# A two-block transformer kernel on one core: the on-chip tensors are stored in another order

## The reference, cut to what matters

```python
act = gelu(einsum('td,ted->te', hx, u_sel))      # u_sel = peer_u[idx]
out = einsum('te,ted->td', gate * act, v_sel)    # v_sel = peer_v[idx]
```

## The kernel before, in words

| tensor | byte | remainder by 256 |
|---|---|---|
| ring | 16,544 | 160 |
| weights_hi | 32,928 | 160 |
| more_lo | 80,032 | 160 |
| u_lo | 162,976 | 160 |
| v_lo, first block | 212,176 | 208 |
| work | 198,752 | 96 |
| small | 206,944 | 96 |
| h | 212,064 | 96 |
| hh | 220,256 | 96 |

## Time and profile before

### The profile page before, as it was taken

The page is one execution under the profiler, slowest core; times in us unless marked ns, Lnnn a source line. Parts: engine busy times, 40 slices in busy tenths (PEclk is TensorE's granted clock), DMA queues, the critical chain, the costliest instruction groups (busy, mean ns, idle before and its releaser), DMA issues.

```text
span 3314.2 us, 71368 instructions
## 1 busy us (share of the span) xinstructions
PE 3191.5 (96%) x28224; PEld 3071.2 (93%) x28224; DVE 2522.3 (76%) x4560; ACT 1604.3 (48%) x2581; POOL 197.1 (6%) x331
## 2 busy tenths in 40 slices
PE   6999989999999999899999999999899999999998
PEld 6999769999967998889999999998789999999998
DVE  7989667988835896748978867776756978877776
ACT  4466644454544445234455444444425455554444
POOL 1100001111100110200000000000400000000000
PEclk9999999999999999999999999999899999999999
DMA  9965218979721993156775477775226885567774
GB/s 392 390 225 168 75 45 329 388 292 371 265 87 49 406 359 124 41 172 201 232 213 171 149 249 235 235 237 167 84 87 193 243 238 174 174 211 236 235 236 161
DMA packets 246737, 707.30 MB, mean 213 GB/s; under 512 B 27488, under 2 KB 93024, under 8 KB 245456
## 3 DMA queue, kind: packets, MB, share of 16 engines
q1 hardware_dynamic: 212256, 572.17, 52.1%
q0 software_dynamic: 34224, 131.55, 10.4%
HBM read 669.00 MB, written 34.60 MB: 212 GB/s over the span
## 4 chain that ended last, share of the span: by engine, by line
PE 88%; DVE 5%; DMA 3%; ACT 2%; issue 1%; SPq 0%; POOL 0%; DVEq 0%; POOLq 0%; ACTq 0%
PE psum L584 39%; PE psum L616 29%; PE psum L1138 3%; PE psum L1073 1%; PE psum L713 1%; DMA ring<-stream 1%; PE psum L965 1%; PE psum L555 1%; PE psum L988 1%; DMA arena<-mod_weights 1%; PE psum L595 1%; PE psum L761 1%; DVE ring L1730 1%; PE psum L596 1%; PE psum L880 1%
## 5 line engine op out<-in xcount | busy, mean ns | idle before, releaser
L584 PE MATMUL psum<-hh,weights_hi 128*128 128x256 f32 x4216 | 1190.1, 282 | 20.0 <-ACT arena L1429 8.5
L584 PE MATMUL psum<-h,weights_hi 128*128 128x256 f32 x4216 | 1175.2, 279 | 0.0
L584 PEld LDWEIGHTS psum<-hh,weights_hi 128*128 128x128 f32 x4216 | 798.1, 189 | 26.6 <-issue 11.2
L584 PEld LDWEIGHTS psum<-h,weights_hi 128*128 128x128 f32 x4216 | 796.8, 189 | 0.2
L616 PE MATMUL psum<-small,weights_hi 128*128 128x256 f32 x2752 | 770.0, 280 | 4.6 <-DVE ring L1730 4.6
L616 PE MATMUL psum<-work,weights_hi 128*128 128x256 f32 x2752 | 768.3, 279 | 0.0
L1730 DVE TENSOR_TENSOR ring<-ring,weights_hi 128x1024 fp32r<-128x1024 f32 x463 | 566.1, 1225 | 184.6 <-ACT weights_hi L1212 180.7
L1212 ACT ACTIVATE weights_hi<-ring 128x1024 fp32r<-128x1024 f32 x463 | 488.3, 1056 | 373.2 <-PE psum L616 182.2
L584 PE MATMUL psum<-hh,ring 128*128 128x256 f32 x2016 | 563.6, 280 | 0.0
L616 PEld LDWEIGHTS psum<-small,weights_hi 128*128 128x128 f32 x2752 | 520.8, 189 | 5.2 <-issue 5.0
L616 PEld LDWEIGHTS psum<-work,weights_hi 128*128 128x128 f32 x2752 | 520.1, 189 | 0.1
(11 more groups left out here) (418 smaller groups left out, 4895.6 us busy)
## 6 DMA issues: line engine op xcount, KB each, us to landing
ring<-stream SPq DMA_DIRECT2D x487, 512.0 KB, 4.4
arena<-stream SPq DMA_DIRECT2D x342, 512.0 KB, 5.3
arena<-mod_weights POOLq DMA_DIRECT2D x224, 512.0 KB, 7.1
v_raw<-stream SPq DMA_DIRECT2D x128, 512.0 KB, 4.8
acts<-small SPq DMA_DIRECT2D x256, 128.0 KB, 3.6
work<-acts SPq DMA_DIRECT2D x256, 128.0 KB, 3.6
arena<-w_uq POOLq DMA_DIRECT2D x1, 3072.0 KB, 10.8
arena<-cond_rows POOLq DMA_DIRECT2D x2, 1024.0 KB, 7.4
```

Of the source, the lines that this page charges most:

```text
L584: mm = pe.matmul(out, lhs[:, d, :], rhs[:, d, :], start=(d == 0 and p == 0), stop=(d == DT - 1 and p == 2))
```

## The change

The order in which tensors are named is changed. `v_raw`/`v_lo`, `ident_bf16`, `h` and `hh` now come directly behind `vfirst`, then `work` and `small`, and the small constants (`cols`, `kept`, `zeros`, `eps`, `modc`, `one_minus_k_a`) last. The V blocks begin at the start of their piece of memory. `ident_bf16` (256 bytes) and a filler of 164 words lie under their first bytes, and `h` starts behind these. No instruction is added, taken away or moved; each reads and writes the same tensors as before.

```diff
--- before.py
+++ after.py
@@ -93,7 +93,7 @@
 
 
 UV_RING = 8
-U_AHEAD, U_AT, V_PAD = 120, 111, 28
+U_AHEAD, U_AT, V_PAD = 120, 111, 228
 
 
 def uv_cycle(l):
@@ -322,6 +322,17 @@
         sb("arena_end", [P, 128 - U_AT - 4 * (UV_RING - RING), 256])
         x = sb("x", [P, DT, T])
         vfirst = sb("vfirst", [P, 4, T])
+        with nc.sbuf_tensor("v_raw", [P, (UV_RING - RING) * 1024], F32) as v_raw:
+            pass
+        with nc.sbuf_tensor("v_lo", [P, (UV_RING - RING) * 1024], F32R) as v_lo:
+            pass
+        IDB = sb("ident_bf16", [P, P], BF16)
+        sb("ahead_of_activations", [P, V_PAD - P // 2])
+        h, (h_lo,) = sb_twice("h", [P, DT, T], [([P, DT, T], F32R)])
+        hh, (h_hi,) = sb_twice("hh", [P, DT, T], [([P, DT, T], F32R)])
+        work, (_, gat_lo) = sb_twice("work", [P, 2048], [([P, 1024], F32), ([P, 4, T], F32R)])
+
+        small, (gat_hi, _) = sb_twice("small", [P, 5, T], [([P, 4, T], F32R), ([P, T], F32)])
         cols = sb("cols", [P, NCOLS])
         kept = sb("kept", [P, KEPT])
         ident, ones, iota, half = (kept[:, i * P:(i + 1) * P] for i in range(4))
@@ -329,17 +340,6 @@
         eps = sb("eps", [P, 20])
         modc = sb("modc", [P, NSUB, 24])
         omk = sb("one_minus_k_a", [P, 8])
-        sb("ahead_of_activations", [P, 2])
-        work, (_, gat_lo) = sb_twice("work", [P, 2048], [([P, 1024], F32), ([P, 4, T], F32R)])
-
-        small, (gat_hi, _) = sb_twice("small", [P, 5, T], [([P, 4, T], F32R), ([P, T], F32)])
-        with nc.sbuf_tensor("v_raw", [P, V_PAD + (UV_RING - RING) * 1024], F32) as v_raw:
-            pass
-        with nc.sbuf_tensor("v_lo", [P, V_PAD + (UV_RING - RING) * 1024], F32R) as v_lo:
-            pass
-        h, (h_lo,) = sb_twice("h", [P, DT, T], [([P, DT, T], F32R)])
-        hh, (h_hi,) = sb_twice("hh", [P, DT, T], [([P, DT, T], F32R)])
-        sb("behind_activations", [P, V_PAD])
 
         ijg, rs, rv = small[:, 0:3, :], small[:, 3, :], small[:, 4, :]
         PS = ctx.enter_context(nc.psum_tensor("psum", [P, 8, 512], F32))
@@ -349,7 +349,7 @@
         SQ = AR[:, 120:128, :]
 
         def v_block(v, s):
-            return v[:, V_PAD + 1024 * (s - RING):V_PAD + 1024 * (s - RING + 1)]
+            return v[:, 1024 * (s - RING):1024 * (s - RING + 1)]
 
         def raw(n):
             s = SLOT[n]
@@ -420,7 +420,6 @@
         MB = flat(h[:, 0:6, :]).rearrange("p (a b) -> p a b", a=2)
         SFR, OHB = gat_lo[:, 0, :], gat_lo[:, 1, 0:64]
         ARG_BANKS = (4, 5, 3, 1)
-        IDB = ctx.enter_context(nc.sbuf_tensor("ident_bf16", [P, P], BF16))
 
         SQH = AR[:, 0:16, :]
         QLAT, KVLAT, LAT = AR[:, 24:27, :], AR[:, 27:29, :], AR[:, 24:29, :]
```

## The result

The changed kernel takes 3367.71 us (median of 4 runs, 3365.35 to 3370.94), the one before 3302.19 us on the same chip (4 runs, 3293.08 to 3316.26). The ratio is 1.0192, 95% interval 1.0162 to 1.0222. My forecast was 3288 us, within 1% of before. The mechanism that came is that of the slower rival.

What follows compares the result with a forecast made beforehand. TensorE's matmul pace, set by how activation and weight addresses meet in SBUF, was taken as the bound. Only mending `v_lo` counted, -16.6 us from the median 3304.19, giving 3287.6, stated as 3288 us; range 3246 to 3395 us.

Steps and rivals of the forecast that it cites:

- the slower rival: Every product in parts: the new difference is a bad one, 3372 us at 117.8 ns to 3420 at 120.0; chance 0.32.
- `v_lo` at the remainder of `ring`: V halves: 128 blocks reading `v_lo` go from 118.7 to 113.3 ns a matmul like ring blocks, -16.6 us.
- Slow stretches as a matter of chance: Long runs at 117.8 ns, about 23 us, vary between executions by how a run starts; taken at nothing on average.
- The price of -96: Other 18,552 matmuls, difference -64 to -96: taken at 113.3 ns, no change; bounds -30 to +144 us over all 21,624.
- the nearest uniform row: Matmuls with one difference, -64, throughout, at 113.3 ns; taken as the pace for -96.
- the nearest in bytes: V half blocks with `v_lo`, difference -112 for it, at 118.7 ns; not taken as the pace for -96.
- the V stretch: V half blocks with `v_lo`, 118.7 ns: two thirds of loads at -64, one at -112; read as two differences in turn.
- a restart of 16 ns at each `v_lo` load: V half: each `v_lo` load loses 16 ns, about one restart behind a pause (0.02 us).
- The bounds of step 3: Pace at -96: from 111.9 ns (fp32 matmuls of 128 columns) to 120.0 ns (difference 0), -30 to +144 us.
- Constants, splits, transfers and the overlay at nothing: Constants moved to the end, splits and transfers hidden behind TensorE, overlay adding no wait: nothing.
- The rival of 912 bytes between `v_lo` and `h`: Filler: `h` starting 912, not 928, bytes behind `v_lo` makes -112 for all, at the slower rival's prices; no separate chance.

Runs made afterwards that it cites:

- oldv64: Kernel before with V_PAD 16 in place of 28, moving `v_lo` from remainder 208 to 160, difference -64 for it too; 3295.18 us, ratio 0.9977.
- again: Kernel before with nothing changed, run once more for its trace; 3312.66 us.
- old96: Kernel before, its old order kept, without 2 words ahead of the activations and with V_PAD 24 for 28, difference -96 everywhere; 3365.31 us, ratio 1.0184.
- n64: Changed kernel with the filler cut from 164 to 48 words, difference -64 everywhere; 3288.57 us, ratio 0.9977 to the kernel before.
- s112: Changed kernel's order, activation tensors cut from one piece entered some words behind its start, difference -112 for all slots; 3372.82 us in one run.
- n0: Changed kernel's order with no filler, activations at remainder 160, difference 0 to all weight slots; 3397.42 us in one run.
- w128: `n64` without the 2 words ahead of the weights, every tensor 32 bytes lower, difference still -64; 3298.11 us, ratio 0.9971 to the kernel before.
- w128a96: Changed kernel without the 2 words ahead of the weights, every tensor 32 bytes lower, difference still -96; 3369.66 us.

## Why the prediction was wrong, by its own steps

The reading of the bound was right: it was the pace of the matmuls that moved, and it moved with the difference of remainders. The clock of the faster pace was read in the earlier trace rows from a window that lies in a V half; in the U half of layer 1, where the pace was 113.3 ns, it was 1.00 too:

```profile
2540.00:2700.00 160.00, 160.00 (x1415) 1.00 0.82 243
```

Each step:
1. `v_lo` at the remainder of `ring`: right that V and ring blocks become alike, and right in size in the traces where the difference stays -64 (16.3 us in `oldv64`). It did not come here because both became slow together.
2. Slow stretches as a matter of chance: right (`again`). At -96 there are two paces as well, 117.3 and 118.7 ns, only close together. The four runs of the changed kernel lie within 5.6 us where those of before spread over 23; but the four of `old96`, with the same two paces, spread over 22, so a narrow spread does not belong to -96.
3. **The price of -96 is the step that failed.** I took 113.3 ns, that of the nearest uniform row, over 118.7 ns, that of the nearest in bytes. Measured: 117.3 and 118.7. Between 113.33 and these, 21,624 matmuls cost 86 to 116 us over the 3276 of a kernel wholly at 113.3 ns, so 3362 to 3392, and 3368 came. The mean of the distances was 118.17 ns; by the sum alone that is 3381. The sum leaves out that pauses shrink: from `n64` (3281.88 us in its profiled execution) to the changed kernel (3370.94) the distances under 130 ns grew by 103 us and the longer ones fell by 14, which is the 89 us between the two. The argument by which I set the V stretch aside was that it was slow because two differences took turns, so that -112 alone would not be. `s112` is against it: with -112 alone and no turns the V halves take 361.96 us or more, 118.7 ns (its starts are 16 bytes off a multiple of 32, as that of `v_lo` before was). The trace of before is against its mechanism too: the loss was spread almost evenly over the three matmuls of a tile (118.9, 118.4, 118.6 ns) and was not a restart of 16 ns at each `v_lo` load. That 16 ns was near the cost of a restart was a coincidence, and it led me astray. Why one load in three at -112 slows all three matmuls is not shown. The bounds of step 3, 111.9 to 120.0 ns, held every pace of the table.
4. and 5. Constants, splits, transfers and the overlay at nothing: right. The Trainium skill ("SBUF — State Buffer", who interferes with whom) allows contention at the port pair shared by VectorE and GpSimd alone, and by that rule too nothing could have changed. The runs disagree: 3397.42 us for n0 against 3288.57 for n64 with the same instructions.

The chances were off in the same place. The choice between the two near rows of step 3 was close to even, and 0.48 against 0.32 leaned to the wrong one. The range ended at 3395 us and held the result. Within the range, the result lay where the slower rival was priced, not where the forecast was. The rival of 912 bytes between `v_lo` and `h` would have been -112, which `s112` has: 3372.82 us in one run, so the rounding to 928 changed little.

**What stays open.** Why just -64 is good is not shown; the runs give a table and no mechanism. They show that the weight load beside a matmul takes part, since moving `v_lo` alone changed the pace. What throws a stretch into its slow pace was not tried. `oldv64` and `n64` have a ratio of 0.9977, about 8 us, where the V halves gain 16 us in their traces, and the interval of `oldv64` ends at 14 us. I suppose that a V half wholly at -64 can fall into the 117.8 ns way in other executions, which two differences in turn (116.1 ns on average) had kept it from. No trace here caught one, so this is not shown.

The best version is thus the kernel before, or the changed one, with -64 for all: `n64`, `oldv64` and `w128` have ratios of 0.9977, 0.9977 and 0.9971 to the kernel before (that of `n64` is not clear of 1) and are 2% below the changed one.

## What to carry to other kernels

Where TensorE is the bound, with fp32r matmuls of 256 columns and a weight load for each, look at the distance of their starts and at the addresses of the two operands before any storage order is changed. Keep the difference of remainders (by 512 bytes to be safe, since the period is little tested), and read it from the built program, since each start is rounded up. A value between two measured ones can't be had by interpolation; try it alone, with an unchanged order, before it is made part of a larger change.

## What the runs showed of the hardware that was not expected

- The pace of matmuls changed with the address of the moving operand (the activations) less the address of the weights, taken by 256 bytes: 113.3 ns in `n64` to 120.0 ns in `n0` for one and the same instruction, 5.9%. Moving both by 32 bytes changed nothing (`w128`, `w128a96`).
- One difference has two stable paces, 113.3 and 117.8 ns at -64. In the U halves a run of 1632 matmuls keeps one throughout (184.97 against 192.22 us), and in `n64`, `oldv64`, `w128` and the changed kernel no pace changed except behind a pause. The profiled executions of `n64` (3281.88 us, mean distance 113.62 ns) and `oldv64` (3300.86 us, 114.51 ns), both wholly at -64, differ by 22 us in the distances under 130 ns and by 19 us in time. No execution of the kernel before near its 3293 us was profiled, so the share of this in its spread of 0.7% is not shown.
- A move of 8 bytes decides: from -64 to -56 it is 3288.57 against 3406.39 us, be it by the difference or by a start that is no multiple of 32.
